# A Strassen MLP on one NeuronCore: other order of products and of VectorE's and ScalarE's work, two outputs begun together

## What is computed

```python
def sqrelu_mlp(h, w_up, w_down):
    return jnp.square(jax.nn.relu(h @ w_up)) @ w_down      # 1024 -> 4096 -> 1024
# x += mixer(rms_norm(x, g));  x += sqrelu_mlp(rms_norm(x, g), w_up, w_down)
```

## Time and profile before

| | us |
|---|---|
| median of 3 runs | 2527.31 (2525.75 to 2528.38) |
| the profiled execution | 2526.19 |
| its span, first to last instruction | 2524.3 |
| PE busy | 2343.8 (93%) |
| DVE busy | 1641.6 (65%) |
| ACT busy | 893.2 (35%) |
| POOL busy | 457.6 (18%) |

### The profile page before, as it was taken

One profiled execution on the slowest core, in us unless ns is written; L12 is line 12 of the kernel. 1 busy time (PEld: TensorE's weight loads), 2 busy tenths in 40 slices (PEclk: granted clock), 3 DMA queues, 4 the chain that ended last, 5 costly groups with the idle time before them and its releaser, 6 DMA issues.

```text
span 2524.3 us, 46083 instructions
## 1 busy us (share of the span) xinstructions
PE 2343.8 (93%) x17433; PEld 2249.6 (89%) x17433; DVE 1641.6 (65%) x2780; ACT 893.2 (35%) x1636; POOL 457.6 (18%) x387
## 2 busy tenths in 40 slices
PE   8999997999998989989999999998989998998998
PEld 8987897998898989989899998887989988998897
DVE  6459536667768776677713326457776779677775
ACT  6459524233324332333410126223332334233332
POOL 1015201221123112211000004011212212221120
PEclk9999998999999999999999999998999999999999
DMA  8530121222322232223321126331232222222322
GB/s 224 79 85 24 47 74 51 84 83 69 106 74 79 71 102 80 83 83 100 106 51 38 56 89 182 131 99 57 84 100 83 83 83 84 83 83 83 100 66 102
DMA packets 183195, 217.39 MB, mean 86 GB/s; under 512 B 34445, under 2 KB 140969, under 8 KB 182940
## 3 DMA queue, kind: packets, MB, share of 16 engines
q1 hardware_dynamic: 180156, 203.23, 26.9%
q0 software_dynamic: 2720, 12.56, 1.6%
q10 hardware_dynamic: 224, 0.30, 0.0%
HBM read 193.61 MB, written 24.47 MB: 86 GB/s over the span
## 4 chain that ended last, share of the span: by engine, by line
PE 65%; DVE 22%; issue 8%; ACT 3%; DVEq 1%; DMA 0%; ACTq 0%
PE ps L1997 25%; PE ps L309 7%; PE ps L312 7%; PE ps L310 7%; PE ps L1955 6%; DVE w_lo L1542 4%; DVE relu L1814 3%; PE ps L1959 3%; DVE relu_sq L1847 2%; DVE relu_sq L1856 2%; DVE w_lo L284 1%; DVE act_lo L1863 1%; DVE relu L1824 1%; PE ps L543 1%; DVE relu L1841 1%
## 5 line engine op out<-in xcount | busy, mean ns | idle before, releaser
L1997 PE MATMUL ps<-act_hi,w_hi 128*128 128x268 f32 (+1 forms) x2048 | 423.9, 288 | 44.2 <-DVE act_lo L1863 44.2
L1997 PE MATMUL ps<-act_hi,w_lo 128*128 128x268 f32 (+1 forms) x2048 | 418.3, 286 | 0.0
L1997 PEld LDWEIGHTS ps<-act_hi,w_hi 128*128 128x128 f32 x2048 | 318.2, 189 | 52.7 <-DVE act_lo L1863 51.4
L1554 POOL TENSOR_TENSOR w_sum<-raw 128x512 f32<-128x512 f32 x128 | 176.9, 1382 | 997.6 <-PE ps L1997 624.5
L1928 DVE TENSOR_TENSOR x<-x,ps 128x536 f32<-128x536 f32 (+1 forms) x256 | 180.8, 706 | 249.7 <-PE ps L1997 249.7
L1997 PEld LDWEIGHTS ps<-act_hi,w_lo 128*128 128x128 f32 x2048 | 318.5, 188 | 0.0
L1959 PE MATMUL ps<-b_lo,w_hi 128*128 128x268 f32 (+1 forms) x1792 | 297.3, 288 | 13.1 <-DVE b_lo L1705 13.1
L1997 PE MATMUL ps<-act_lo,w_hi 128*128 128x268 f32 (+1 forms) x2048 | 303.9, 286 | 0.0
L1955 PE MATMUL ps<-b_hi_low,w_hi 128*128 128x268 f32 (+1 forms) x1024 | 267.0, 290 | 22.0 <-DVE w_lo L1542 20.5
L1538 ACT ACTIVATE w_hi<-w_sum 128x512 fp32r<-128x512 f32 x256 | 153.9, 627 | 366.0 <-POOL w_sum L1554 366.0
L1955 PE MATMUL ps<-b_hi_high,w_hi 128*128 128x268 f32 (+1 forms) x768 | 209.2, 301 | 75.2 <-DVE relu L1829 65.3
(11 more groups left out here) (360 smaller groups left out, 4362.6 us busy)
## 6 DMA issues: line engine op xcount, KB each, us to landing
raw<-in_mlp_w_up SPq DMA_DIRECT2D x64, 1024.0 KB, 5.7
raw<-in_mlp_w_down SPq DMA_DIRECT2D x64, 1024.0 KB, 5.0
raw<-in_mlstm_w_in SPq DMA_DIRECT2D x12, 1024.0 KB, 5.5
x<-scratch_x SPq DMA_DIRECT2D x8, 537.0 KB, 6.0
scratch_x<-x POOLq DMA_DIRECT2D x1, 4296.0 KB, 12.0
x<-scratch_x SPq DMA_DIRECT2D x8, 528.0 KB, 5.5
x_tok<-in_x_prompt SPq DMA_DIRECT2D x8, 512.0 KB, 7.8
raw<-in_attn_w_qkv SPq DMA_DIRECT2D x16, 256.0 KB, 6.6
```

What stands on the lines that cost most here:

```text
L1554: nc.gpsimd.tensor_tensor(dst, in0, in1, op).then_inc(w_summed, 1)
L1997: last = nc.tensor.matmul(ps[:, bank + g, 0:q], wk, act[:, k, q * g:q * g + q], start=start, stop=stop)
```

## The change

- The products of a pair are renumbered: items 2 and 3 trade places in PE's order, and items 5 and 6 too. Step 1 now needs the fourth product (it needed the third); steps 8 to 10 finish the pair's *second* block of hidden units, steps 11 to 13 the first. Item 5 waits for step 2 (was 4), item 6 for step 4.
- The weights' splits come in the order 0, 1, 2, 4, 3, 6, 5, in other slots (`PART_OF`); POOL's fourth sum for pair 1 waits for four products (was six).
- DVE's and ACT's lists in a run are reordered accordingly.
- `mlp_down_pe` begins outputs 0 and 1 both with pair 0's blocks (24 matmuls), then gives each its blocks 3 and 2; further outputs take the blocks in the order 1, 0, 3, 2.
- Rows' factors, first half: the low parts of items 0 and 1 are made ahead of the last addition of the projection, and the rest in another order; `norm_pe` comes after the fourth product (was the third); ACT makes factors 4 to 6 ahead of `norm_rstd_act` (was after).
- Rows' factors, second half: the four sums go from DVE to POOL (`b_half_pool`), behind POOL's last sum of the up-projection and ahead of its sums for the next run; ACT and DVE get one high and one low part at each output.

```diff
-        ITEMS = (0, 1, 3, 4, 2, 5, 6)
+        ITEMS = (0, 1, 2, 4, 3, 6, 5)
...
+        PART_OF = ((0, 1, 2, 3, 4, 6, 5), (0, 1, 2, 3, 4, 5, 7))
...
-            dst = w_part(w_sum, (1, 2, 3, 5)[k])
-            in0, in1, op = ((a21, a22, ALU.add), (s1, a11, ALU.subtract), (a11, a21, ALU.subtract),
+            dst = w_part(w_sum, pair, (1, 2, 3, 6)[k])
+            in0, in1, op = ((a21, a22, ALU.add), (a11, a21, ALU.subtract), (s1, a11, ALU.subtract),
                             (a12, s2, ALU.subtract))[k]
...
             for k in range(4):
-                pool.wait_ge(up_ready, ups((2, 3, 4, 6)[k]))
+                pool.wait_ge(up_ready, ups((2, 3, 4, 4)[k]))
                 sum_pool(pool, 1, k, sums(4))
+            if last_of_half:
+                b_half_pool(pool, layer, ups)
...
+        def b_half_pool(pool, layer, ups):
+
+            pool.wait_ge(b_by_dve, b_count(layer, 1, 7))
+            pool.wait_ge(b_by_act, b_count(layer, 1, 7))
+            pool.wait_ge(up_ready, ups(14))
+            for k in range(4):
+                b_sum(pool, nc.gpsimd, layer, 1, k)
...
                 if c == KC - 2:
-                    b_dve(dve, m // 2, 0, 0)
+                    b_sum(dve, nc.vector, m // 2, 0, 0)
+                if c == KC - 1:
+                    b_lo_dve(dve, m // 2, 0, 0)
+                    b_lo_dve(dve, m // 2, 0, 1)
                 dve.wait_ge(x_back[c], 32)
                 add_x_dve(dve, n0 + c, c, x, m)
...
+            b_sum(dve, nc.vector, m // 2, 0, 1)
+            b_sum(dve, nc.vector, m // 2, 0, 2)
+            b_lo_dve(dve, m // 2, 0, 2)
             norm_acc_dve(dve, m, KC - 1)
...
             if then == "half":
+                act.wait_ge(b_summed, 1 + b_count(layer, 1, 4))
                 for f in range(KC):
                     b_scale_act(act, layer, 1, f, x)
                 act.wait_ge(up_ready, mlp_ups(layer, half, i)(14))
                 b_hi_act(act, layer, 1, 0)
-                b_hi_act(act, layer, 1, 1)
...
             up_lo_dve(dve, 1, 0, w(7 + 1))
-            take(0, 1, 2, 3, 4, 5, 6, 7)
-            dve.wait_ge(w_summed, sums(6))
+            take(0, 1, 2, 3, 4, 5)
+            dve.wait_ge(w_summed, sums(7))
             up_lo_dve(dve, 1, 1, w(7 + 2))
-            up_lo_dve(dve, 1, 3, w(7 + 3))
+            take(0, 6, 7)
+            up_lo_dve(dve, 1, 2, w(7 + 3))
+            take(0, 8, 9, 10)
             up_lo_dve(dve, 1, 4, w(7 + 4))
-            take(0, 8, 9, 10)
+            act_lo_dve(dve, layer, 0, 1, taken, acts)
+            take(0, 11, 12, 13)
+            up_lo_dve(dve, 1, 3, w(7 + 5))
+            up_lo_dve(dve, 1, 6, w(7 + 6))
             act_lo_dve(dve, layer, 0, 0, taken, acts)
...
-            up_lo_dve(dve, 1, 6, w(7 + 7))
-            take(1, 1)
+            up_lo_dve(dve, 1, 5, w(7 + 7))
+            take(1, 1, 2, 3, 4)
             mlp_down_lo(dve, 0, w(15))
-            take(1, 2, 3, 4, 5, 6, 7)
+            take(1, 5, 6, 7)
             mlp_down_lo(dve, 1, w(16))
             take(1, 8, 9, 10)
+            act_lo_dve(dve, layer, 1, 1, taken, acts)
+            take(1, 11, 12, 13)
             act_lo_dve(dve, layer, 1, 0, taken, acts)
...
-                    elif item == 5:
-                        pe.wait_ge(up_taken, taken(13 * pair + 4))
+                    else:
+                        pe.wait_ge(up_taken, taken(13 * pair + (2 if item == 5 else 4)))
                     product_pe(pe, layer, half, pair, item, bank, w)
-                    if first and pair == 0 and item == 2:
+                    if first and pair == 0 and item == 3:
                         for g in range(3):
                             norm_pe(pe, 2 * layer + 1, g)
...
+            pe.wait_ge(w_lo_ready, w(14 + 1))
+            pe.wait_ge(up_taken, taken(11))
+            pe.wait_ge(act_split, acts(2))
+            blocks(0, (1, 0))
+            blocks(1, (1, 0))
+            for o in range(2):
+                for count, k in ((3, 3), (4, 2)):
+                    pe.wait_ge(act_split, acts(count))
+                    last = blocks(o, (k,))
+                last.then_inc(out_ready, 1)
+            for o in range(2, 8):
```

More of the change, by code:

```diff
@@ new lines, in b_hi_act, with b_lo_dve @@
+            else:
+                act.wait_ge(b_summed, 1 + b_count(layer, half, 4) + {1: 1, 2: 2, 3: 3, 5: 4}[j])
+            nc.scalar.activation(b_hi(layer, j), b_factor(layer, j), ACT.Copy).then_inc(b_by_act, 1)
+        def b_lo_dve(dve, layer, half, j):
+            dve.wait_ge(b_by_act, b_count(layer, half, 7) + j + 1)
+            nc.vector.tensor_tensor(b_lo(layer, j), b_factor(layer, j), b_hi(layer, j).bitcast(F32), ALU.subtract
+                                    ).then_inc(b_by_dve, 1)
@@ L1800, in mlp_run_act @@
                     mlp_next_hi_act(act, layer, half, i, o)
-                    if then == "half" and 2 <= o < 7:
-                        b_hi_act(act, layer, 1, o)
+                    if then == "half" and o < 6:
+                        b_hi_act(act, layer, 1, o + 1)
         def up_take_dve(dve, layer, half, i, pair, step, ups, taken):
             q, first, second = up_views(layer, pair)
-            x0, z0, y0, y1 = (up_bank(layer, pair, w)[:, 0:q] for w in range(4))
+            x0, z0, y1, y0 = (up_bank(layer, pair, w)[:, 0:q] for w in range(4))
             m1, m2 = relu[0], relu[1]
@@ L1937, in mlp_run_dve @@
                     mlp_next_lo_dve(dve, layer, half, i, o)
-                    if then == "half":
-                        for step in {0: (2,), 1: (3,), 2: (4,), 3: (5,), 4: (6,), 5: (7,), 6: (8, 9), 7: (10,)}[o]:
-                            b_dve(dve, layer, 1, step)
+                    if then == "half" and o:
+                        b_lo_dve(dve, layer, 1, o - 1)
             if then == "norm":
@@ L1954, in product_pe @@
                 for n, w in enumerate((w_hi, w_lo)):
-                    nc.tensor.matmul(o, w_part(w, item)[:, k, :], hi[:, k, :], start=k == 0 and n == 0,
+                    nc.tensor.matmul(o, w_part(w, pair, item)[:, k, :], hi[:, k, :], start=k == 0 and n == 0,
                                      stop=False)
-            pe.wait_ge(b_by_dve, by_dve + (2, 3, 7, 8, 9, 10, 11)[item])
+            pe.wait_ge(b_by_dve, b_count(layer, half, 7) + item + 1)
             for k in range(4):
-                last = nc.tensor.matmul(o, w_part(w_hi, item)[:, k, :], lo[:, k, :], start=False, stop=k == 3)
+                last = nc.tensor.matmul(o, w_part(w_hi, pair, item)[:, k, :], lo[:, k, :], start=False, stop=k == 3)
             last.then_inc(up_ready, 1)
@@ L1965, in mlp_up_pe @@
             for pair in range(2):
-                for item, bank in ((0, 0), (1, 1), (2, 2), (3, 3), (4, 0), (5, 1), (6, 3)):
+                for item, bank in ((0, 0), (1, 1), (2, 2), (3, 3), (4, 0), (5, 2), (6, 1)):
                     if item in (0, 1, 2, 3):
@@ new lines, in blocks @@
+            def blocks(o, ks):
+                for k in ks:
+                    passes(o, k, w_hi, act_hi, k == 1, False)
+                    passes(o, k, w_lo, act_hi, False, False)
+                for k in ks:
+                    last = passes(o, k, w_hi, act_lo, False, k == 2)
+                return last
+            pe.wait_ge(w_lo_ready, w(14 + 1))
[3 more added lines that the diff above has]
+            blocks(1, (1, 0))
```

283 lines of the change are left out of this document (118 added, 165 removed).

## The result

The changed kernel takes 2483.33 us (median of 4 runs, 2480.90 to 2486.69), the kernel before 2526.83 us on the same chip (2525.75 to 2528.38). The ratio is 0.983, with an interval of 0.981 to 0.985: 1.7% less. The forecast was 2476 in a range of 2450 to 2505. The profiled execution has a span of 2483.0 us against 2524.3, so 41.3 us are to be explained; the prediction had 51.4.

A forecast was written before the change was run, and what follows sets the result against it. A chain of PE's products, DVE's list and PE's remaining matmuls was taken to bound each ordinary run. 2526.2 - 36.4 (ordinary runs) - 20 (first runs) + 5 (half runs) = 2474.8; median 1.1 higher: 2476 us, range 2450 to 2505.

The forecast's parts named there:

- The run as a chain: Ordinary MLP run: PE's four products 6.24, DVE's list 21.2, hand-over 0.77, PE's rest 20.1; 48.3 us, 1.3 less.
- the last term: What PE has left after the last act_lo: 162 matmuls instead of 174, 20.1 us, 1.5 us less.
- rival D: PE reaches the down-projection after pair 1's act_lo, so ordinary runs' gain shrinks towards 0; 12% together with rival A.
- The lock: POOL's sum holds DVE operations with two SBUF inputs; the fourth sum meets step 5, which takes 1.2 to 1.4 us.
- rival A: POOL's sum holds DVE's chain twice per run, or a late split costs 1.3 us; 2515 us; 12% with D.
- The failed step: Layers' first runs, ahead of step 1: norm reached at 12.2 us, step 1 at about 17.0; both runs together -20.
- Ends of halves: Run after each change of half: step 1 about 9.5 us late (4 to 13); +5 us in all.
- the causes named: Change of half: POOL's late weight sum holds ACT, low part 2 holds DVE, then DVE has some 11 us of work.
- The last run of layer 0: Counted as an ordinary run, so forecast to gain 1.3 us.
- rival C: PE's closer waits in ordinary runs halve its clock for 5 us, losing 2.5 us each; 2546 us; 6%.

The follow-up runs named there:

- kernel with the one edit: The kernel before, with only outputs 0 and 1 of the down-projection both begun with pair 0's blocks, all other orders kept; 2484.25 us, ratio 0.983.

## Why the prediction was right, and where it was off

**The run as a chain** held in each of its terms, to 0.1 us: 6.21, then DVE's list until 27.36, 0.77, and 20.0 us of PE for 162 matmuls, 48.13 against 48.3. The runs with the second output left out (174 matmuls left, 49.65) and with 12 matmuls added ahead of the last `act_lo` (49.62) show the last term by itself, and those without POOL's fourth sum (47.20) and with the squares on ACT (45.51) the second.

**What was needed for it** was misjudged. The prediction asked whether PE would be at the down-projection in time, and gave rival D to that; it never asked whether the old order would do. The kernel with the one edit shows that PE comes just in time in the old order as well, with no wait for `act_lo` and so nothing to spare, while in the changed kernel it waits 1.39 us there. Rival D did not happen in either. So the gain of ordinary runs comes from one of the listed changes; the others have none of their own there.

**The lock** was placed and priced right (1.36 us for step 5), and rival A, a second operation held in each run, did not occur. In first runs POOL's sums are done by step 1, as the prediction said: step 5 takes 0.43 us (415.35), and the rest behind step 1 was right (60.26 - 19.26 = 41.0 against 42.1 - 1.0 = 41.1). The failed step lies ahead of step 1, where the sum has nothing for the same POOL sums beside DVE's: 2.0 us of holding, as I read it, and a clock that was at half during the norm. First runs gained 16.3 us and not 20.

**Ends of halves.** Step 1 of the next run is 10.0 us late in the first layer (809.39 - 745.05 = 64.3 from the start of the run before, against 48.1 + 6.2) and 7.3 in the second (2088.49 - 2027.32 = 61.2, against 47.7 + 6.2), where 9.5 was forecast for both. The pairs cost +5.3 us for +2.4, and 3.1 of that are a fall of the clock behind the last `act_lo` of each second run (832.10 and 2112.10), which the forecast doesn't have and the kernel before neither. Of the causes named, that POOL's order costs time is shown by the run that moves the weight sum first; that it does so by ACT's wait behind `w_summed` is not, since step 1 hardly moved there. Against the kernel with the one edit the cost is larger, 9.5 us, since it has the gain of the ordinary run in these runs too.

**The last run of layer 0** was counted with the ordinary ones and gained nothing. What follows it is DVE's addition and norm. Timelines of PE, the first matmuls of the gates behind it, in the kernel after:

```profile
1194.83 7.88 PE L2119 MATMUL ps<-x,wg_raw 128*8 128x358 f32 x48 [3.18 <-DVE x L1922]
```

in the kernel with the one edit:

```profile
1193.40 5.00 PE L2127 MATMUL ps<-x,wg_raw 128*8 128x358 f32 x48 [2.80 <-DVE x L1928]
```

and in the kernel before:

```profile
1213.21 4.99 PE L2118 MATMUL ps<-x,wg_raw 128*8 128x358 f32 x48 [1.31 <-DVE x L1928]
```

The 1.5 us that PE is earlier turn into a longer wait for DVE (1.31 to 2.80 and 3.18), so nothing is gained there; and in the kernel after the clock is at half from 1193.9 on, within the wait, and the 48 matmuls take 2.9 us more.

**The clock**, rival C, was given 6%. In the changed kernel it took 3 us in ordinary runs (two of 49.65 where others take 48.13), 3.1 behind the changes of half and the 2.9 above, 9 us for which the forecast has nothing. As a mechanism it is real: without the second begun output it costs 40 us more than the chain says (2570 for 2530). The count of ordinary runs with a fall, of 24 each: before 0, one edit 0, after 2, weight sum first 1, low parts back 3, without the fourth sum 8, redundant matmuls 16, without the second output 22, squares on ACT 0.

Together: -41.2 against -51.4. Of the difference of 10.2 us, 3.7 are the first runs, 2.9 the pairs of runs (5.3 for 2.4), 4.2 the end of layer 0's MLP and 1.8 the stretch ahead of the MLP; ordinary runs went 2.2 better, in spite of the two falls. No large errors cancel in the total: ordinary runs alone erred the other way.

**What stays open** is why the clock falls in one ordinary run and not in the next, when both have the same waits to 0.1 us; three waits of 0.72, 1.65 and 1.40 us never did it, 1.27, 0.34 and 1.39 did twice in 24, and 0.36, 0.31 and 1.41 eight times. Nor is it shown why the low parts moved back cost about as much behind step 1 as ahead of it, nor what of the loss at the ends of halves is POOL's order.

## What to carry to other kernels

Find the chain that a stretch consists of, across engines, before pricing an edit: here removing waits of 65 us by itself was worth nothing, and filling those of 44 us carried the gain. Where one engine waits for another's last result, look for work that needs only early results and begin more of it ahead of the wait; that was a small edit and all of the gain. Sums moved to POOL are paid back by DVE where its operations have two SBUF inputs, and what a shorter list gives can be taken back in part by PE's clock (12 of 22 us without POOL's fourth sum, nothing with the squares on ACT), so count the falls before and after.

## What the runs showed of the hardware

- PE's clock fell to 0.50 for 3.4 us and more behind single waits all under 2 us (1.30, 1.79 and 1.40 us within 14 us, or even 0.36, 0.31 and 1.41), in runs in which PE was busy 91% and more of the time.
- With the wait of 1.79 us filled down to 0.33, the clock fell in 16 of 24 ordinary runs and not in 22, and the kernel was 23 us faster with 384 more matmuls.
- A DVE operation on two SBUF inputs of 1072 elements took 3.60 us for 1.27 beside POOL's sum of the same size (2.86), and one of 268 elements 1.36 for 0.43.
